# Splitting the sums of squares into one TensorE job per element, and a cap on consecutive small work in a list scheduler

## The reference, cut to what matters

```python
proj = h @ w_in                        # h is [512, 1024]
q = rms_norm(q, q_gain)                # per head of 64:
k = rms_norm(k, k_gain)                #   x * rsqrt(mean(x*x) + eps) * gain
s = einsum(q, k) * 64 ** -0.5 + bias   # then softmax, then p @ v
merged = sum over branches of sigmoid(gate) * (branch @ w_branch)
```

## Time and profile before

| | us |
|---|---|
| median of 3 runs | 3172.18 |
| lowest, highest run | 3170.93, 3176.06 |
| span of the profiled execution, first to last instruction | 3168.3 |
| TensorE busy in that span | 2986.7 (94%) |
| mean granted TensorE clock | 0.958 |
| first stream, about | 118 to 526 |
| second stream, about | 2206 to 2717 |

### The profile page before, as it was taken

One profiled execution on the slowest core, in us unless ns is written; L12 is line 12 of the kernel. 1 busy time (PEld: TensorE's weight loads), 2 busy tenths in 40 slices (PEclk: granted clock), 3 DMA queues, 4 the chain that ended last, 5 costly groups with the idle time before them and its releaser, 6 DMA issues. The chain is left out here.

```text
span 3168.3 us, 46409 instructions
## 1 busy us (share of the span) xinstructions
PE 2986.7 (94%) x18622; PEld 2400.4 (76%) x18622; DVE 2114.6 (67%) x2176; ACT 1587.1 (50%) x1767; POOL 278.6 (9%) x225
## 2 busy tenths in 40 slices
PE   5999999789999999999999968997999999999999
PEld 4777787468888888888887746887778887778877
DVE  6567754569998999999999964566453344356642
ACT  3556433357777777777777633223443442333321
POOL 0110010001111111111111100332000000000000
PEclk9999999789999999999999978998999988999999
DMA  6322343369999999999999942001222112323321
GB/s 248 123 84 88 102 153 109 121 246 373 370 370 376 379 369 374 371 370 378 376 369 369 363 163 67 4 4 39 72 61 60 57 57 78 107 80 93 94 91 68
DMA packets 217373, 607.95 MB, mean 192 GB/s; under 512 B 10785, under 2 KB 118305, under 8 KB 183425
## 3 DMA queue, kind: packets, MB, share of 16 engines
q1 hardware_dynamic: 202480, 554.87, 47.7%
q0 software_dynamic: 14592, 50.36, 4.7%
q10 hardware_dynamic: 144, 0.53, 0.1%
HBM read 582.62 MB, written 23.10 MB: 191 GB/s over the span
## 5 line engine op out<-in xcount | busy, mean ns | idle before, releaser
L2472 DVE TENSOR_TENSOR weight_ring_part<-weight_ring,weight_ring_part 128x2048 fp32r<-128x2048 f32 x380 | 853.4, 2288 | 103.7 <-ACT weight_ring_part L2411 103.2
L2411 ACT ACTIVATE weight_ring_part<-weight_ring 128x2048 fp32r<-128x2048 f32 x380 | 713.3, 1914 | 256.0 <-PE ps L193 138.2
L193 PE MATMUL ps<-weight_ring_part 128*128 128x512 f32 x1456 | 583.7, 401 | 0.0
L293 DVE TENSOR_TENSOR weight_ring_part<-weight_ring,weight_ring_part 128x2048 fp32r<-128x2048 f32 x111 | 253.2, 2281 | 238.3 <-ACT weight_ring_part L290 235.9
L189 PE MATMUL ps<-weight_ring_part,gathered_hi 128*128 128x512 f32 x1024 | 408.9, 399 | 0.0
L193 PE MATMUL ps<-weight_ring_part,gathered_hi 128*128 128x512 f32 x1024 | 405.2, 396 | 0.0
L192 PE MATMUL ps<-weight_ring_part,gathered_lo 128*128 128x512 f32 x1024 | 405.1, 396 | 0.0
L189 PE MATMUL ps<-h1T_hi,weight_ring_part 128*128 128x512 f32 x872 | 363.0, 416 | 3.1 <-DVE weight_ring_part L293 1.7
L192 PE MATMUL ps<-h1T_hi,weight_ring_part 128*128 128x512 f32 x872 | 351.5, 403 | 0.0
L193 PEld LDWEIGHTS ps<-weight_ring_part 128*128 128x128 f32 x1456 | 280.1, 192 | 70.6
L290 ACT ACTIVATE weight_ring_part<-weight_ring 128x2048 fp32r<-128x2048 f32 x111 | 211.1, 1901 | 133.8 <-PE ps L193 103.6
(11 more groups left out here) (491 smaller groups left out, 4466.5 us busy)
## 6 DMA issues: line engine op xcount, KB each, us to landing
weight_ring<-in_w SPq DMA_DIRECT2D x190, 2048.0 KB, 8.6
weight_ring<-in_w_in SPq DMA_DIRECT2D x58, 1024.0 KB, 5.4
weight_ring<-in_w_ffn_up SPq DMA_DIRECT2D x44, 512.0 KB, 5.0
weight_ring<-in_w_ffn_down SPq DMA_DIRECT2D x11, 1024.0 KB, 4.8
mod_tile<-in_w_ada POOLq DMA_DIRECT2D x36, 256.0 KB, 3.2
weight_ring<-in_w_ada SPq DMA_DIRECT2D x8, 1024.0 KB, 13.0
gate_rows<-in_w_ada POOLq DMA_DIRECT2D x28, 256.0 KB, 3.2
weight_ring<-in_w_branch SPq DMA_DIRECT2D x6, 1024.0 KB, 5.8
```

Source lines behind the costliest of these rows:

```text
L193: return nc.tensor.matmul(out, x[0], y[1], start=False, stop=stop)
L293: self.nc.vector.tensor_tensor(lo, full, hi, ALU.subtract).then_inc(self.split, 1)
L2411: nc.scalar.activation(hi_half(h), full_half(h), ACT.Copy).then_inc(w_rounded, 1)
L2472: nc.vector.tensor_tensor(lo_half(h), full_half(h), hi_half(h), ALU.subtract).then_inc(w_split, 1)
```

## The change: what it does

1. `sums` of a batch becomes one job `sum` for each element of the batch, planned at 0.9 us each instead of 1.8 us for the batch. The instructions are the same. The first of a batch carries the waits, the last one signals. Between them the shared bank stays held, so other users of the bank can't come between, but products and attention jobs can.
2. The planner keeps a counter for TensorE, `small_work`: a job that isn't a product adds its length, a product takes off 1.5 times its length. Once the counter is at 1.0 or more, TensorE's next job is a product, if one can start within 0.5 us of the soonest job of any kind.

```diff
-job(("sums", b), "pe", 1.8, 2, *[("square", e) for e in batch["elements"]], ("sums", b - 1) if b else None)
-job(("root", b), "act", 2.0, 0, ("sums", b), ("factors", b - 2) if b >= 2 else None)
+for j in range(len(batch["elements"])):
+    job(("sum", b, j), "pe", 0.9, 2, *([("square", e) for e in batch["elements"]] if j == 0 else []),
+        ("sum", b, j - 1) if j else last_sum(b - 1) if b else None)
+job(("root", b), "act", 2.0, 0, last_sum(b), ("factors", b - 2) if b >= 2 else None)
...
+small_work, most_small = 0.0, 1.0
...
-            if name[0] in spare_users and holder is not None:
+            found = []
+            if name[0] in spare_users and holder is not None and not (name[0] == "sum" and name[2]):
...
+            found.append(((start, jobs[name][2], at, len(orders[engine])), name, engine, start))
+        if engine == "pe" and small_work >= most_small and found:
+            soon = min(x[3] for x in found) + 0.5
+            found = [x for x in found if x[1][0] == "prod" and x[3] <= soon] or found
...
+    if engine == "pe":
+        small_work = max(0.0, small_work - 1.5 * jobs[name][1]) if name[0] == "prod" else small_work + jobs[name][1]
...
-def sums(b):
-    pe.wait_ge(squared, squared_at[batches[b]["elements"][-1]])
-    take_spare(rooted, sums_before["sums", b] + 1)
-    for j, e in enumerate(batches[b]["elements"]):
-        for t in range(TT):
+def sum_(b, j):
+    e = batches[b]["elements"][j]
+    if j == 0:
+        pe.wait_ge(squared, squared_at[batches[b]["elements"][-1]])
+        take_spare(rooted, sums_before["sum", b] + 1)
+    for t in range(TT):
...
+    if j == len(batches[b]["elements"]) - 1:
+        last.then_inc(summed, 1)
```

More of the change, by code:

```diff
@@ L941, in lay_out @@
             last = lambda e: ("prod", e, steps_of[e] - 1)
+            last_sum = lambda b: ("sum", b, len(batches[b]["elements"]) - 1)
             by_kind = lambda kind: [e for e, x in enumerate(elements) if x["kind"] == kind]
@@ L958, in lay_out @@
                     b = batch_of[e]
-                    job(("square", e), "act", 0.7, 1, last(e), ("out", e - 1) if e else None, ("sums", b - 1) if b else None,
+                    job(("square", e), "act", 0.7, 1, last(e), ("out", e - 1) if e else None, last_sum(b - 1) if b else None,
                         *([("spread", b - 1, len(batches[b - 1]["keys"]) - 1)] if b and batches[b - 1]["keys"] else []))
@@ L1032, in lay_out @@
                     job(("mod_out", g), "act", 0.7, 1, ("mod_sum", g))
-            spare_users = {"mod_sum": "mod_out", "turn_v": "v_copy", "sums": "root", "spread": "scale", "sub_sums": "sub_root", "sub_out": "sub_mul"}
+            spare_users = {"mod_sum": "mod_out", "turn_v": "v_copy", "sum": "root", "spread": "scale", "sub_sums": "sub_root", "sub_out": "sub_mul"}
             waiting = {name: len(needs) for name, (_, _, _, needs) in jobs.items()}
@@ L1055, in lay_out @@
                         start = max(at, free[engine])
-                        key = (start, jobs[name][2], at, len(orders[engine]))
-                        if best is None or key < best[0]:
-                            best = (key, name, engine, start)
+                        found.append(((start, jobs[name][2], at, len(orders[engine])), name, engine, start))
+                    if engine == "pe" and small_work >= most_small and found:
+                        soon = min(x[3] for x in found) + 0.5
+                        found = [x for x in found if x[1][0] == "prod" and x[3] <= soon] or found
+                    for x in found:
+                        if best is None or x[0] < best[0]:
+                            best = x
                 _, name, engine, start = best
                 del ready[engine][name]
-                if name[0] in spare_users:
-                    holder = (spare_users[name[0]],) + name[1:]
+                if engine == "pe":
+                    small_work = max(0.0, small_work - 1.5 * jobs[name][1]) if name[0] == "prod" else small_work + jobs[name][1]
+                if name[0] in spare_users and not (name[0] == "sum" and name[2]):
+                    holder = (spare_users[name[0]],) + (name[1:2] if name[0] == "sum" else name[1:])
                 free[engine] = ended[name] = start + jobs[name][1]
@@ L1094, in stream @@
             for step in order["pe"]:
-                if step[0] in ("sums", "sub_sums"):
-                    sums_before[step] = len(sums_before)
+                if step[0] == "sub_sums" or step[0] == "sum" and step[2] == 0:
+                    sums_before[step[0:2]] = len(sums_before)
             with stage("group_ready", "bank_free0", "bank_free1", "squared", "summed", "rooted", "factors_ready", "spread_ready",
@@ L1195, in turn_v @@
                         last.then_inc(v_turned, 1)
-                    def sums(b):
-                        pe.wait_ge(squared, squared_at[batches[b]["elements"][-1]])
-                        take_spare(rooted, sums_before["sums", b] + 1)
-                        for j, e in enumerate(batches[b]["elements"]):
-                            for t in range(TT):
[L1202 to L1205, removed]
+                    def sum_(b, j):
[4 more added lines that the diff above has]
+                        for t in range(TT):
+                            at = 8 * j + 2 * t
+                            last = nc.tensor.matmul(ps[:, 2, at:at + 2], sq[:, slot_of_square(e), elements[e]["tokens"](t)], head_sum[:, 0:P:HD],
+                                                    start=True, stop=True)
+                        if j == len(batches[b]["elements"]) - 1:
+                            last.then_inc(summed, 1)
                     def spread(b, j):
@@ L1294, in _ @@
                             turn_v(*n)
-                        elif kind == "sums":
-                            sums(*n)
+                        elif kind == "sum":
+                            sum_(*n)
                         elif kind == "spread":
@@ L1319, in square @@
                         if b:
-                            act.wait_ge(summed, sums_before["sums", b - 1] + 1)
+                            act.wait_ge(summed, sums_before["sum", b - 1] + 1)
                             if batches[b - 1]["keys"]:
@@ L1362, in square_root @@
                         m = 8 * len(batches[b]["elements"])
-                        act.wait_ge(summed, sums_before["sums", b] + 1)
+                        act.wait_ge(summed, sums_before["sum", b] + 1)
                         if b >= 2:
@@ L1466, in sums @@
                         m = 8 * len(batches[b]["elements"])
-                        dve.wait_ge(rooted, sums_before["sums", b] + 1)
+                        dve.wait_ge(rooted, sums_before["sum", b] + 1)
                         if b >= 2 and batches[b - 2]["keys"]:
```

## The result

| | before | changed |
|---|---|---|
| median, us | 3172.93 (4 runs) | 3186.31 (4 runs) |
| lowest, highest | 3170.93, 3176.06 | 3181.83, 3193.14 |
| profiled span | 3168.3 | 3180.0 |

The ratio is 1.0046, 95% interval 1.0032 to 1.0060: the change makes the kernel 10 to 19 us slower. The forecast was no change, 3171.2 in a range up to 3181.

The account below looks back on a forecast made before the run. The prediction took both streams to be bound by TensorE and its clock, which falls at the sums. Its terms, -6.5 + 3.5 - 1.0 + 2.5 + 0.5 = -1.0 us, gave 3171.2 us, range 3160 to 3181.

Parts of the forecast that it names:

- The cap on other small work: Both streams: products beside turns, weighs and scores win nothing; 0, with both ends at 4 us either way.
- second stream with no wait: Sign of being right: TensorE still has no wait in the second stream of the changed profile.
- I let about half of the gain turn into waits there: 3.5 us.: First stream: products run out sooner before source 0, so TensorE waits there; 3.5 us given back.
- the gain of 6.5 us: First stream's three full batches of sums: alternation with products wins 1.5 us at the first, 2.5 at each other.
- most there is to win: Time lost to the low clock at the ten batches of sums in both streams: 29 us, 0.9% of the kernel.
- the natural batches keep the clock in alternation: Full natural-order batches, both streams: products between sums partly hold the clock; 6.5 us won in the first, 1.0 in the second.
- rival 1: Alternation holds the clock at all natural batches, and at stepped ones after their first pair; 10 to 20 us won, chance 0.27.
- the stepped batches: Second stream's four stepped batches: first two sums still lower the clock, products between prolong it; +0.6 each, 2.5 us lost.
- Rival 2: Clock stays low through the whole alternation at nine full batches; 11 to 15 us more, 3179 to 3184, chance 0.18.
- Rival 3: No effect: the clock isn't about the sums, or gains are waited away before source 0; 3172, chance 0.10.
- The rule on idle gaps: Only gaps in which TensorE idles lower its clock, so mixing products between sums would be worth nothing; given a small chance.
- five falls at scores: Second stream's stepped scores lost the clock five times, 1.5 us each; dips changing by over 4 us would show it wrong.

Follow-up runs that it names:

- `spread_mixed`: Kernel before, sums still one job per batch, with the cap acting only while a weight spread is ready; 3181.32 us, ratio 1.0029.
- `sums_second_long`: The change with the cap only before second-stream sums, and stepped query sums of batches 2 to 5 planned at 1.8 us; 3147.41 us, ratio 0.9922 against before.
- `fast_spread_mixed`: `sums_second_long` with the cap also acting before the weight spreads; 3162.88 us, ratio 0.9965 against the kernel before.
- `spread_free`: The change, but the cap doesn't hold while a weight spread is ready; 3172.17 us, ratio 1.0006 against the kernel before.

## Why the prediction was wrong

**The step that failed: the term "The cap on other small work", put at "0, with both ends at 4 us either way".** The prediction lists turns, weighs and scores as the other small work and leaves out the 12 weight spreads: planned at 0.9 us each like a sum, rank 1, in a row, the longest run of small work in either stream. Its rows of the second stream end at 2598 and never reach them, though the trace of before has them as a block of 17 us, 13 of it with the clock at 0.50. The block did little harm because nothing but spreads stood in it. The cap put 9 products into it, and the "second stream with no wait" got one of 4.9 us. That is worth 13 to 14 us by two pairs of runs, where the term had 0.

The ratios of the runs add up to the whole: the split with its length wins 0.0030 (9.5 us), the cap in the first stream costs 0.0033 (10.5), the cap at the spreads 0.0040 (12.7). Together 13.7 us slower; measured are 14.6. Without the spreads it would have been 1.0006, inside the forecast range, but by luck: a gain that the prediction didn't know of and a cost three times its own would have cancelled.

**Second failing, a term right in kind and too small: what the cap costs in the first stream.** "I let about half of the gain turn into waits there: 3.5 us." The waits came nearly as forecast (4.5 us, five of them; forecast 5 to 7), if not all at their place. But the gain of 6.5 us that stood against them isn't there on the whole, since the clock falls elsewhere instead, and the runs put the cap in this stream at 10 us against the same split without it. Of this the waits explain 4; the rest isn't settled. That the stretch from 118 us to the end of the stream got 2.3 us shorter in the profile (forecast 3) says nothing: in single profiles the stream's length differs by 6 us for one and the same order of instructions (before and `spread_mixed`, 411.7 and 405.4). The two have 24 and 10 us at 0.50 in it up to 300, and 14 x 0.45 is those 6 us.

**That scatter is also in the price of the sums.** The 29 us "most there is to win" were read from one execution. With the 3.4 us that `spread_mixed` has at each full batch of the first stream, and none at the half batch, the same order gives 23 us. One reading under it was not what it was called: at 2545 to 2547 the last batch is at its natural sums, so that window doesn't show a stepped sum at 0.50. `sums_second_long` does, and bears out that it takes as long as at 1.00.

**What I had not considered at all:** the planned length of the sums. The prediction takes the new 0.9 for a detail of the split. The length is worth 5 us without any split, and the split without it nothing.

**Right in part: the natural batches keep the clock in alternation.** In this execution all five full ones hold 1.00, which is 3.1 us each in the first stream, where the prediction had 1.5 and 2.5, and 1.5 each in the second, where it had 0.5. For the three that begin with one sum the other profiles agree (16 of 16). For the two that begin with a pair it was luck (4 of 11); that the first batch should win only half was the better guess. The ten batches had 40 us at 0.50, between the forecast (53) and rival 1 (under 30).

**Right in sign, small in size: the stepped batches.** "+0.6 each, 2.5 us lost": 3 us more at 0.50 in the two profiles, 1.4 us lost, which is within what single profiles differ by. With the pair together and products behind it the stepped batches fell in 16 of 16 (four profiles); with the stepped sums apart and longer planned they held in 6 of 8 (`sums_second_long` and `fast_spread_mixed`; the same batch fell in both). Whether the parting or the second product does it isn't separated.

**Rival 2** had the side and nearly the time, for another place. Its mechanism, a stretch that stays low for as long as the small work in it lasts and makes the products inside it slow, is what happened, but at the spreads, not at nine batches. At the natural sums that begin with a pair it is right in 7 of 11 cases, at the others wrong. **Rival 1** holds for the natural batches that begin with one sum. **Rival 3** falls in its first half, that the clock has nothing to do with the sums: without products between them 41 of 43 natural batches fell, with one sum at a time none of 16. Its second half, that what is won is waited away, is close to what the first stream shows. The rule on idle gaps (Trainium skill, TensorE: Matmul & The Clock Gate, section Why this matters for your kernels) doesn't cover the falls at the sums and at the spreads; TensorE was busy throughout there, before and after.

**Chance:** five falls at scores became one (at 2391.9), about 6 us, and most of the 5.6 us by which the changed kernel is ahead at the first mark. `spread_free`, with the same order up to the spreads, has four of them. The prediction names this as a sign of being wrong and says that it can't foresee it.

## What to carry to other kernels

A rule added to a scheduler acts on every job that meets its condition, so list the jobs by planned length and rank before you price the rule; the one that hurts is the one that the rule wasn't written for. Work that lowers TensorE's clock should stand in a block if nothing else has to stand in it, or be thinned by enough products that the clock never falls; the mixture in between is the worst, because the products then run at half speed too. And first give the planner true lengths: here that was worth 5 us by itself, and 13 us, together with the cap in front of the sums, for two elements whose strided reads take twice as long as their neighbours'. Where the clock can fall or hold in one and the same order, read several profiles before you call it held.

## What the runs showed of the hardware

- TensorE's clock held 1.00 in 16 of 16 batches in which one sum (0.9 us of two-column matmuls) was followed by a product (0.7 us) before the next sum, in 4 of 11 that began with two sums, and in 2 of 43 without products between. It fell in 16 of 16 where two stepped sums (3.7 us) stood together, and held in 6 of 8 where these stood singly, with one and two products behind them.
- The 12 spreads (fp32, 8 rows by 512 columns, two passes) in one block left 17 us at 0.50, in them and behind them (20 in one of the ten profiles). With nine products (three matmuls, 1.6 us from the start of one to the next spread) between them it was 34 us in three profiles and 31 in the fourth; the products didn't bring the clock back.
- A sum over squares read with a step of four fp32 takes 1.8 us at 1.00, twice the natural 0.95, and 1.8 at 0.50 (2411.11 in `sums_second_long`), where the natural one takes 1.70: step and half clock don't add up.
- The same order of instructions had 24 us at 0.50 up to 300 in the first stream of one execution and 10 in that of another (before and `spread_mixed`), and was 6 us longer.
- The mean clock of a kernel doesn't rank close kernels (0.959 was slower than 0.958 in the profiled pair): what counts as well is which work stands in the low stretches. Among the 17 executions of the kernel before on one chip it does follow the time: 0.964 in the fastest (3157.8 us), 0.956 in the slowest (3176.5).
